# Identity matmuls in TensorE's pauses: around the chunk stage, the meta tile and the first pair of the up projection

## The chip, the cores and the metric

The kernel runs on one core of a Trainium2 chip. The metric is the device time in microseconds; the kernel before took 3239.58 us, the median of 3 runs from 3239.42 to 3240.31. A change of the time under 0.2% (6.5 us) is about what such a measurement can't tell from none.

## The reference, cut to what matters

A decoder block over 16 meta tokens and 2048 tokens of width 1024, all in float32:

```
hn   = rms_norm(h, norm_mix_pre)
proj = hn @ w_in                                   # rwkv fields, s5 input, gates
y_a  = rwkv7(p_rwkv) @ w_branch                    # a recurrence over the tokens, 8 heads of 64
y_b  = s5(u_s5) -> glu
mix  = (gate_a * y_a + gate_b * y_b) @ w_out
h    = h + rms_norm(mix, norm_mix_post)
hn   = rms_norm(h, norm_ffn_pre)
up   = hn @ ffn_w_up                               # 1024 x 5632
f    = (gelu(causal_conv(up[:, :2816])) * up[:, 2816:]) @ ffn_w_down
h    = h + rms_norm(f, norm_ffn_post)              # the 16 meta rows are dropped
```

The change leaves all of this as it is. What it adds is multiplied into PSUM places that nothing reads.

## The kernel before, in words

The program has one instruction stream for each engine; semaphores order them, and the loops are unrolled by hand at their ends. Large matmuls have their operands split in a high and a low part (float32r) and take three products, hi x hi, hi x lo, lo x hi. Small ones, and TensorE's transposes with the identity `ident` (128x128, float32), work in plain float32.

The stages, with the stretch of the profile that each takes:

- the input projection (`norm_in_projection`, to 958 us), which ends with a gate tile: weight tiles against all tokens, small matmuls of the rwkv fields and of the s5 scan between them. `tile_loop` is its loop; its last argument is a tail.
- the chunks (`rwkv_chunks`, 959 to 1427 us): the recurrence in 33 chunks of 64 tokens, two at a time in 17 steps. TensorE's part first prepares chunk 0 alone: `grams_of`, `gram_l`, `turn_toks`, a transpose `turn_x1`, a product `lx`, and then `levels`, in which `xq`, `turn_x` and `lx` alternate, each waiting for VectorE or ScalarE to copy or scale what the one before put into PSUM. Then comes step 0, written out (it has chunk preparations of both lanes, `pres`, and one main chunk), a loop over 15 steps, and a last step with no preparations (`if not pres`), in which `main_...` products and transposes of the result (`turn_y`) wait for VectorE and ScalarE in turn.
- the mix of the two branches (`branch_mix`, from 1428 us); its first products are of the chunk stage's result, and VectorE multiplies each with a gate, at L2322.
- the output projection (`token_projection`, to 1918 us), in row tiles of 128 tokens and at last a meta tile of 16. `turn` transposes a normed row tile, for the next stage.
- the up projection (`ffn_up`, from 1919 us), by pairs of weight tiles. Each pair is seven products, `for step in range(7)`, in the order P_1, P_2, P_6, P_7, P_4, P_5, P_3; in the first phase each has three units of 258, 256 and 512 columns, of 12 matmuls each. In the first pair VectorE and ScalarE still split the activations (L2999 and L3152) while TensorE works. After the first pair come 10 more of that phase, then the second phase, then the down projection.

Three things set the order around the change. TensorE takes its instructions in order: a matmul that is put ahead of a waiting one delays it if it lasts longer than the wait. A block of the program (`nc.Block()`) ends when every engine has drained (DRAIN in the profile, which ends with the engine's last instruction), and behind it `stage_ends` clears semaphores behind a second barrier (L3711 and L3713). And several lines that the prediction speaks of belong to one helper: L1537 is `products`, L1543 is `turns`, L1565 is `grams_of`, L2567 is `turn`, L2966, L2969 and L2972 are the three products of a unit of up.

```
mm = T_.transpose(psum[:, first + b, place * WIDE:(place + 1) * WIDE], src(b), ident)      # turns
mm = nc.tensor.matmul(psum[0:H, 4, g * P:(g + 1) * P], b_s[:, g, :], out_1[:, g, 0:C * H], start=True, stop=True)   # tables, L544
```

Of the kernel before, what the change touches and what calls it, by code (L numbers as in the profile page):

```python
# [28 lines left out]
P = 128  # L29
# [58 lines left out]
TWO_PI_PARTS = two_pi_parts()  # L88

# [12 lines left out]
def norm_in_projection(nc, name, sems, psum, src, gain_rows, x_hi, x_lo, weight, consts, w_tiles, mu, s5_small, s5_bc, s5_tab, s5_u, s5_y, rwkv_out, gate_out, ident, pre,  # L102
# [42 lines left out]
    with ExitStack() as ctx:  # L145
# [357 lines left out]
        def _(pe):  # L503
# [201 lines left out]
            tile_loop(pe, tile, lambda: None, gate_tile, lambda: None)  # L705
# [602 lines left out]
def rwkv_chunks(nc, name, sems, psum, prep, v_dram, chunk_decay, masks_dram, bonus_dram, gate_dram, cols, y_hi, y_lo, last_roles_stored, store_last_y, last_y_stored, ident, next_loads, next_split):  # L1308
# [13 lines left out]
    with ExitStack() as ctx:  # L1322
# [182 lines left out]
        def _(pe):  # L1505
# [165 lines left out]
            def step(g, mains, pres):  # L1671
# [4 lines left out]
                has_pb = not isinstance(g, int) or g >= 1  # L1676
                if not pres:
                    main_y_state(g, 0, flat_copied(a - 2))
                    main_u(g, 0)
                    main_m(g, 0, ALL)  # L1680
                    main_y_values(g, 0, ALL)
                    main_w_values(g, 1)
                    main_w_state(g, 1)
                    turn_y(pb, copied(y_ready, a))
                    main_y_state(g, 1, flat_copied(pb))
                    main_u(g, 1)
                    main_y_values(g, 1, ALL)
                    turn_y(a, copied(y_ready, b))
                    turn_y(b, flat_copied(a))
                    return  # L1690
# [18 lines left out]
                if has_a:  # L1709
                    main_m(g, 0, ALL)  # L1710
                lx(*place[0], 0)
                if has_a:
                    main_y_state(g, 0, toks_copied(1))
                turn_x1(*place[1])
                if has_a:
                    main_y_values(g, 0, ALL)
                lx(*place[1], 0)
# [31 lines left out]

            pe.wait_ge(masks_loaded, 16)  # L1750
# [3 lines left out]
            chunk_0 = (1, 0)  # L1754
            turn_x1(*chunk_0)
            lx(*chunk_0, 0)
            levels({1: chunk_0}, lambda l, chain: None, FIRST_LEVELS)
# [596 lines left out]
def token_projection(nc, name, sems, psum, acts, first_col, w_dram, k_tiles, passes, gain, residual, out, out_first, meta_tile, next_norm=None, early=None, begun=None):  # L2354
# [23 lines left out]
    with ExitStack() as ctx:  # L2378
# [169 lines left out]
        def _(pe):  # L2548
            pe.sem_inc(k_done, k_tiles)
            for part in range(passes):  # L2550
# [11 lines left out]
                def turn(s, r, u, i, n, token):  # L2562

                    pe.wait_ge(row_normed, r + 1 + SLOTS)
                    pe.wait_ge(turned_out, r + 1)
                    for k in range(KD):
                        mm = nc.tensor.transpose(psum[:, 4 + 2 * u + k // 4, k % 4 * P:k % 4 * P + n], row_normed_buf[0:n, u, k * P:(k + 1) * P], ident[0:n, 0:n])  # L2567
                    mm.then_inc(turned, 1)

                if next_norm:  # L2570
                    pe.sem_inc(turned, SLOTS)
                    products(0, 0, 0, 0, P, 0)
                    pe.wait_ge(*mix_banks_free)
                    tiles(pe, products, turn, part)
                else:
                    tiles(pe, None, products, part)
# [149 lines left out]
def ffn_up(nc, block, name, sems, psum, x_space, x_raw, w_raw, w_sets, x_rest, x_sums, conv_w, conv_b, hidden_out, ahead):  # L2726
# [13 lines left out]
    with ExitStack() as ctx:  # L2740
# [206 lines left out]
        def _(pe):  # L2947
            pe.sem_inc(c21_done, 3)
            pe.sem_inc(c12_done, 3)

            def pair(phase, m, first, last, extra):
                g, u0, n = pair_of(phase, m), units_before(phase, m), n_units(phase)
                for step in range(7):
                    for v, part, c0, c1 in units(phase):
# [6 lines left out]
                        cols = slice(c0 - first_column(phase), c1 - first_column(phase))  # L2961
                        pe.wait_ge(freed, count)
# [716 lines left out]
def hybrid_block(nc, ins, out):  # L3679
# [18 lines left out]
    with ExitStack() as ctx:  # L3698
# [54 lines left out]
        with ExitStack() as both:  # L3753
# [4 lines left out]
            with ExitStack() as inner:  # L3758
# [42 lines left out]
                with nc.Block() as block:  # L3801
                    up_done = ffn_up(nc, block, "up", sems, psum, x_space, x_raw, up_weight, ins["w_up_sets"], h_normed, up_sums,
                                     cols[:, COL["conv_w"]:COL["conv_w"] + CONV_W * M_FF], cols[:, COL["conv_b"]:COL["conv_b"] + M_FF], hidden,
                                     (first_set_loaded, held_a, held_b, hidden_sums, down))
                    ffn_down(nc, block, "down", sems, psum, down, *up_done, ins["ffn_post"], h1, out)
# [66 lines left out]
```

## Time and profile before

| | |
|---|---|
| median of 3 runs | 3239.58 us |
| profiled execution, its own time | 3237.82 us |
| its span, first to last instruction | 3236.0 us |
| TensorE busy | 3081.9 us, 95% |
| TensorE weight loads busy | 2751.7 us, 85% |
| VectorE, ScalarE, GpSimd busy | 1986.8, 1346.1, 114.5 us |
| mean granted TensorE clock | 0.984 |

The span and the time differ by 1.8 us, which lie around the first and last instruction. TensorE's share of busy time is the modelled length of its matmuls, which overlap. The clock that TensorE is granted has two levels in this trace, 1.00 (2.4 GHz) and 0.50 (1.2 GHz); at the half level each column takes twice the time. The mean of 0.984 is made of eleven stretches at 0.50 within the span and one at its end.

### The profile page before, as it was taken

The numbers are of one execution on the slowest core, as the hardware profiler recorded it, in microseconds if no ns is written. First come the engines' busy times: TensorE is split into PE (matmuls) and PEld (weight loads), VectorE is DVE, ScalarE is ACT, GpSimd is POOL, SyncE is SP. The second block draws the span as 40 slices with busy tenths as digits, with TensorE's granted clock in tenths as the row PEclk, the third lists the DMA queues.
The fourth block names the chain that finished last, engine by engine and source line by source line (L and its number), as shares of the span: only waits on it lengthen the run. The fifth ranks groups of instructions, "written<-read, shape, count | busy, mean of one in ns | idle before, by whom it ended". The sixth has DMA issues, their size and how long they took to land. (4 is left out here: it accounts for less than half of the span.)

```text
span 3236.0 us, 69046 instructions
## 1 busy us (share of the span) xinstructions
PE 3081.9 (95%) x25426; PEld 2751.7 (85%) x25426; DVE 1986.8 (61%) x3726; ACT 1346.1 (42%) x2373; POOL 114.5 (4%) x120
## 2 busy tenths in 40 slices
PE   8999999999987888869999979999999999999999
PEld 7999999999976777759998868999988888788877
DVE  7676655655654666654345467666687767645576
ACT  6211127667662444441113335444454444433333
POOL 0000000000001222210000000000000000000000
PEclk9999999999998999989999989999999999999999
DMA  5343346566553343333345723333354444666785
GB/s 160 112 140 120 125 154 199 188 199 192 187 149 74 88 100 91 94 116 130 127 143 177 225 101 101 108 108 106 98 166 125 125 126 120 199 219 223 246 308 188
DMA packets 448438, 481.91 MB, mean 149 GB/s; under 512 B 145552, under 2 KB 370704, under 8 KB 444352
## 3 DMA queue, kind: packets, MB, share of 16 engines
q1 hardware_dynamic: 447264, 480.30, 47.4%
q8 instruction: 71, 1.16, 0.2%
q14 instruction: 47, 0.39, 0.0%
q10 hardware_dynamic: 1056, 0.07, 0.0%
HBM read 315.36 MB, written 164.89 MB: 148 GB/s over the span
## 5 line engine op out<-in xcount | busy, mean ns | idle before, releaser
L3480 PE MATMUL psum<-down_w_parts,down_a_hi 128*128 128x512 f32 x1232 | 382.2, 391 | 6.9 <-DVE down_a_lo L3587 6.9
L2966 PE MATMUL psum<-up_x,up_w_hi 128*128 128x512 f32 (+2 forms) x1540 | 353.7, 352 | 12.1 <-ACT up_w_hi L2987 7.0
L2972 PE MATMUL psum<-up_x,up_w_hi 128*128 128x512 f32 (+2 forms) x1540 | 352.8, 351 | 0.8 <-DVE up_x L3152 0.8
L2969 PE MATMUL psum<-up_x,up_w_lo 128*128 128x512 f32 (+2 forms) x1540 | 351.9, 351 | 0.0
L2966 PEld LDWEIGHTS psum<-up_x,up_w_hi 128*128 128x128 f32 x1540 | 260.4, 190 | 53.7 <-issue 7.1
L2969 PEld LDWEIGHTS psum<-up_x,up_w_lo 128*128 128x128 f32 x1540 | 260.5, 190 | 40.7
L2972 PEld LDWEIGHTS psum<-up_x,up_w_hi 128*128 128x128 f32 x1540 | 260.0, 190 | 41.3 <-DVE up_x L3152 1.1
L3480 PEld LDWEIGHTS psum<-down_w_parts,down_a_hi 128*128 128x128 f32 x1232 | 232.3, 189 | 56.9 <-issue 8.7
L697 PE MATMUL psum<-x_hi,proj_w_hi 128*128 128x416 f32 (+1 forms) x640 | 245.1, 383 | 0.0
L3480 PE MATMUL psum<-down_w_parts,down_a_lo 128*128 128x512 f32 x616 | 240.7, 391 | 0.0
L580 PE MATMUL psum<-x_hi,proj_w_hi 128*128 128x416 f32 (+1 forms) x640 | 224.7, 351 | 0.0
L697 PE MATMUL psum<-x_lo,proj_w_hi 128*128 128x416 f32 (+1 forms) x640 | 223.6, 349 | 0.0
L580 PE MATMUL psum<-x_hi,proj_w_lo 128*128 128x416 f32 (+1 forms) x640 | 223.4, 349 | 0.0
L580 PE MATMUL psum<-x_lo,proj_w_hi 128*128 128x416 f32 (+1 forms) x640 | 223.4, 349 | 0.0
L697 PE MATMUL psum<-x_hi,proj_w_lo 128*128 128x416 f32 (+1 forms) x640 | 223.2, 349 | 0.0
L3135 DVE TENSOR_TENSOR up_w_lo<-up_weight,up_w_hi 128x512 fp32r<-128x512 f32 x176 | 118.9, 686 | 93.8 <-ACT up_w_hi L2987 93.8
L3587 DVE TENSOR_TENSOR down_a_lo<-down_raw,down_a_hi 128x1408 fp32r<-128x1408 f32 x54 | 87.7, 1624 | 123.0 <-ACT down_a_hi L3511 122.9
L3511 ACT ACTIVATE down_a_hi<-down_raw 128x1408 fp32r<-128x1408 f32 x54 | 74.5, 1380 | 175.0 <-PE psum L3480 142.9
L2987 ACT ACTIVATE up_w_hi<-up_weight 128x512 fp32r<-128x512 f32 x176 | 109.7, 624 | 85.0 <-PE psum L2972 78.7
L814 ACT ACTIVATE proj_pre<-psum 128x416 f32<-128x416 f32 (+1 forms) x70 | 36.1, 517 | 258.6 <-PE psum L580 204.1
L2987 ACT ACTIVATE up_w_hi<-up_t_sums 128x512 fp32r<-128x512 f32 x132 | 82.8, 629 | 138.7 <-PE psum L2972 129.5
L3480 PEld LDWEIGHTS psum<-down_w_parts,down_a_lo 128*128 128x128 f32 x616 | 116.4, 189 | 24.4
(422 smaller groups left out, 6533.2 us busy)
## 6 DMA issues: line engine op xcount, KB each, us to landing
down_raw<-scratch_hidden SPq DMA_DIRECT2D x48, 704.0 KB, 6.3
scratch_hidden<-up_hidden SPq DMA_DIRECT2D x44, 512.0 KB, 3.2
up_weight<-in_w_up_sets SPq DMA_DIRECT2D x42, 512.0 KB, 4.7
up_weight<-in_w_up_sets SPq DMA_DIRECT2D x84, 256.0 KB, 3.5
proj_scan_area<-scratch_s_tab SPq DMA_DIRECT2D x32, 608.5 KB, 3.9
scratch_s_tab<-proj_area SPq DMA_DIRECT2D x16, 1089.0 KB, 4.3
proj_weight<-in_w_in_tiles SPq DMA_DIRECT2D x33, 512.0 KB, 4.5
down_raw<-scratch_hidden_sums SPq DMA_DIRECT2D x24, 704.0 KB, 5.7
```

Of the source, the lines that this page charges most:

```text
L580: mm = nc.tensor.matmul(psum[:, PRODUCT_BANKS[n], 0:WIDTHS[n]], w[:, v, k, :], x[:, k, block_of(n)], start=(k == 0 and w is w_hi and x is ...
L697: mm = nc.tensor.matmul(psum[:, GATE_BANKS[n], 0:WIDTHS[n]], w[:, v, k, :], x[:, k, block_of(n)], start=(k == 0 and w is w_hi and x is x_h ...
L814: nc.scalar.activation(pre[:, 2 + STARTS[n]:2 + STARTS[n] + WIDTHS[n]], done, ACT.Copy).then_inc(evacuated, 1)
L2966: nc.tensor.matmul(out, w_hi[:, q % 7, k, :], x_hi(phase, step)[:, k, cols], start=opens and k == 0, stop=False, skip_group_check=True)
L2969: nc.tensor.matmul(out, w_lo[:, q % 7, k, :], x_hi(phase, step)[:, k, cols], start=False, stop=False, skip_group_check=True)
L2972: mm = nc.tensor.matmul(out, w_hi[:, q % 7, k, :], x_lo(phase, step)[:, k, cols], start=False, stop=closes and k == K4 - 1, skip_group_che ...
L2987: nc.scalar.activation(w_hi[:, q % 7], weight_of(part, step), ACT.Copy).then_inc(w_hi_ready, 1)
L3135: V.tensor_tensor(w_lo[:, q % 7], weight_of(part, step), w_hi[:, q % 7].bitcast(F32), ALU.subtract).then_inc(w_lo_ready, 1)
L3480: return nc.tensor.matmul(bank, a[:, q % SLOTS, k, :], w(step_of(q), k), start=opens, stop=closes, skip_group_check=True)
L3511: nc.scalar.activation(a_hi[:, q % SLOTS], raw(q, 0), ACT.Copy).then_inc(acts_hi, 1)
L3587: V.tensor_tensor(a_lo[:, q % SLOTS], raw(q, 0), a_hi[:, q % SLOTS].bitcast(F32), ALU.subtract).then_inc(acts_lo, 1)
```

## The change

One helper, `turn_over`, issues `n` matmuls of the identity by itself: 128 rows, 128 columns, float32. It is called

- as the tail of the projection's loop: 22
- at the start of the chunk stage: 28; behind `turn_toks` of chunk 0: 14; behind its `turn_x1` and `lx`: 4 each; and 4 behind each of the eight calls of `fill` in `levels`
- in step 0 alone (where `has_a` is false): 6, 8 and 6
- in the last step of the chunks: 4, 9, 4, 4, 6, 18 and 32
- ahead of the meta tile's transposes: 42, and behind them, as the last of the output projection: 16
- at the start of up: 18, and in its first pair ahead of the fourth product (P_1 + 3, which is P_7), unit 0: 20

There is no new wait, no DMA, and nothing on other engines.

```diff
+def turn_over(nc, out, ident, n):
+
+    for _ in range(n):
+        nc.tensor.matmul(out, ident, ident, start=True, stop=True)
...
-            tile_loop(pe, tile, lambda: None, gate_tile, lambda: None)
+            tile_loop(pe, tile, lambda: None, gate_tile, lambda: turn_over(nc, psum[:, ROLE_BANKS[0], 2 * P:3 * P], ident, 22))
...
+                between = lambda n: turn_over(nc, psum[:, 0, 2 * P:3 * P], ident, n)
+                first_idle = lambda n: turn_over(nc, psum[:, WUM_BANKS, 2 * P:3 * P], ident, n)
                 if not pres:
                     main_y_state(g, 0, flat_copied(a - 2))
                     main_u(g, 0)
+                    between(4)
                     main_m(g, 0, ALL)
                     main_y_values(g, 0, ALL)
                     main_w_values(g, 1)
                     main_w_state(g, 1)
+                    between(9)
                     turn_y(pb, copied(y_ready, a))
+                    between(4)
                     main_y_state(g, 1, flat_copied(pb))
                     main_u(g, 1)
+                    between(4)
                     main_y_values(g, 1, ALL)
+                    between(6)
                     turn_y(a, copied(y_ready, b))
+                    between(18)
                     turn_y(b, flat_copied(a))
+                    between(32)
                     return
...
                 if has_a:
                     main_m(g, 0, ALL)
+                else:
+                    first_idle(6)
                 lx(*place[0], 0)
                 if has_a:
                     main_y_state(g, 0, toks_copied(1))
+                else:
+                    first_idle(8)
                 turn_x1(*place[1])
                 if has_a:
                     main_y_values(g, 0, ALL)
+                else:
+                    first_idle(6)
                 lx(*place[1], 0)
...
+            between = lambda n: turn_over(nc, psum[:, 0, 2 * P:3 * P], ident, n)
+            between(28)
             pe.wait_ge(masks_loaded, 16)
             grams_of(1, 0)
             gram_l(1)
             turn_toks(1)
             chunk_0 = (1, 0)
+            between(14)
             turn_x1(*chunk_0)
+            between(4)
             lx(*chunk_0, 0)
-            levels({1: chunk_0}, lambda l, chain: None, FIRST_LEVELS)
+            between(4)
+            levels({1: chunk_0}, lambda l, chain: between(4), FIRST_LEVELS)
...
                 def turn(s, r, u, i, n, token):
 
+                    if n < P:
+                        turn_over(nc, psum[:, 3, 0:P], ident, 42)
                     pe.wait_ge(row_normed, r + 1 + SLOTS)
                     pe.wait_ge(turned_out, r + 1)
...
                     tiles(pe, products, turn, part)
+                    turn_over(nc, psum[:, 3, 0:P], ident, 16)
...
             pe.sem_inc(c12_done, 3)
+            turn_over(nc, psum[:, 7, 0:P], ident, 18)
...
+                        if first and phase == FIRST and step == P_1 + 3 and v == 0:
+                            turn_over(nc, psum[:, 7, 0:P], ident, 20)
                         pe.wait_ge(freed, count)
```

## Rows read from the trace of the kernel before

**Rows 1.** Windows cut at the clock's changes: length, busy of each engine, clock, DMA.

```profile
991.42:1005.07 13.65, 12.46 (x290) 10.63 (x284) 3.19 (x11) 3.07 (x8) 0.00 (x0) 0.50 0.39 81
...
1032.38:1035.79 3.41, 3.41 (x74) 2.96 (x73) 0.86 (x3) 2.07 (x6) 0.00 (x0) 0.50 0.14 31
...
1414.67:1431.74 17.07, 6.65 (x46) 5.61 (x47) 7.41 (x18) 10.87 (x27) 0.00 (x0) 0.50 0.14 42
```

**Rows 2.** Float32 matmuls: by line (ns min/median/max), timeline (start us, us, records).

```profile
L544 PE MATMUL psum<-proj_area x64: 272/273/283, 118.4 to 450.0; 128*16 128x128 f32 x64
...
118.36 0.61 PE L544 MATMUL psum<-proj_area 128*16 128x128 f32 x4
...
954.24 0.60 PE L568 MATMUL psum<-proj_scan_area 128*128 128x258 f32 x2
```

**Rows 3.** Drain (ns; first, last start); timeline at the chunks' start (bracket: idle before).

```profile
L145 SPq DRAIN  x1: 7/7/7, 957.8 to 957.8; - x1
...
959.21 1.28 ACT L1911 ACT_TABLE_LOAD   x1 [3.05 <-PEq L3713]
...
964.29 1.99 PE L1565 MATMUL psum<-chunk_pre 64*64 64x128 f32 x32 [9.45 <-DMA chunk_pre<-scratch_roles]
...
969.95 0.44 PE L1543 MATMUL psum<-ident_sb,chunk_x 128*128 128x128 f32 x2 [2.03 <-DVE chunk_x L1784]
...
980.98 1.99 PE L1565 MATMUL psum<-chunk_pre 64*64 64x128 f32 x32 [0.47 <-PEq L1760]
```

**Rows 4.** Timeline of TensorE: step 0 of the chunks, and a step of the loop.

```profile
990.04 0.44 PE L1543 MATMUL psum<-ident_sb,chunk_x 128*128 128x128 f32 x2 [1.67 <-DVE chunk_x L1784]
991.04 0.43 PE L1537 MATMUL psum<-chunk_x,chunk_l_t 64*64 64x32 f32 x16 [0.56 <-ACT chunk_x_t L1928]
...
1011.08 1.10 PE L1565 MATMUL psum<-chunk_pre 64*64 64x128 f32 x32
...
1204.42 0.43 PE L1537 MATMUL psum<-chunk_x,chunk_l_t 64*64 64x32 f32 x16 [0.59 <-ACT chunk_x_t L1928]
...
1220.00 1.10 PE L1565 MATMUL psum<-chunk_pre 64*64 64x128 f32 x32
```

**Rows 5.** End of the chunks and start of the mix: timeline, and a drain.

```profile
1405.29 0.59 PE L1537 MATMUL psum<-chunk_m,chunk_ar 64*64 64x64 f32 x11 [5.85 <-issue]
...
1407.02 0.51 PE L1537 MATMUL psum<-chunk_toks_held 64*64 64x64 f32 x8 [0.61 <-ACT chunk_u L1943]
...
1420.85 0.69 PE L1543 MATMUL psum<-ident_sb,chunk_y_unit 128*128 128x128 f32 x2 [2.54 <-DVE chunk_y_unit L1846]
...
L1322 DVEq DRAIN  x1: 458/458/458, 1425.9 to 1425.9; - x1
...
1432.59 0.59 DVE L2322 TENSOR_TENSOR mix_mixed<-psum,mix_gate 128x416 f32<-128x416 f32 x1 [6.24 <-PE psum L2231]
```

**Rows 6.** The meta tile: timeline, and the drains that end its block.

```profile
1906.66 1.03 PE L2567 MATMUL psum<-ident_sb,mixout_row_normed_buf 128*128 128x128 f32 x8
...
1913.74 1.03 PE L2567 MATMUL psum<-ident_sb,mixout_row_normed_buf 16*128 16x16 f32 x8 [6.04 <-DVE mixout_row_normed_buf L2686]
...
L3779 PEldq DRAIN  x1: 1058/1058/1058, 1913.8 to 1913.8; - x1
...
L3779 SPq DRAIN  x1: 7/7/7, 1918.2 to 1918.2; - x1
```

**Rows 7.** The first pair of up: timeline, and one window (columns as in Rows 1).

```profile
1924.63 1.23 PE L2972 MATMUL psum<-up_x,up_w_hi 128*128 128x258 f32 x4 [0.83 <-DVE up_x L3152]
...
1940.61 1.23 PE L2966 MATMUL psum<-up_x,up_w_hi 128*128 128x258 f32 x4 [2.89 <-ACT up_a_pre L3008]
...
1947.79 0.65 PE L2966 MATMUL psum<-up_x,up_w_hi 128*128 128x258 f32 x4
...
1967.21 0.90 PE L2966 MATMUL psum<-up_x,up_w_hi 128*128 128x258 f32 x4 [2.22 <-DVE up_a_pre L3172]
...
1930.00:1940.00 10.00, 7.72 (x45) 6.48 (x43) 9.91 (x9) 3.32 (x4) 0.00 (x0) 1.00 0.00 0
```

More of the change, by code:

```diff
@@ L2723, in _, with ffn_up @@
                     channels_out(TILES, 0, TILES // 2, N_META)
-def ffn_up(nc, block, name, sems, psum, x_space, x_raw, w_raw, w_sets, x_rest, x_sums, conv_w, conv_b, hidden_out, ahead):
+def ffn_up(nc, block, name, sems, psum, ident, x_space, x_raw, w_raw, w_sets, x_rest, x_sums, conv_w, conv_b, hidden_out, ahead):
     first_set_loaded, held_a, held_b, hidden_sums, down = ahead
@@ L3801, in hybrid_block @@
                 with nc.Block() as block:
-                    up_done = ffn_up(nc, block, "up", sems, psum, x_space, x_raw, up_weight, ins["w_up_sets"], h_normed, up_sums,
+                    up_done = ffn_up(nc, block, "up", sems, psum, ident, x_space, x_raw, up_weight, ins["w_up_sets"], h_normed, up_sums,
                                      cols[:, COL["conv_w"]:COL["conv_w"] + CONV_W * M_FF], cols[:, COL["conv_b"]:COL["conv_b"] + M_FF], hidden,
```

## The prediction

> **What bounds the kernel now.** I read the page first: a span of 3236.0 us beside an own time of 3237.82 us, with TensorE busy for 95% of it. TensorE is the bound nearly everywhere, so two things matter: where it pauses, and where its clock is at the half level. The second I read from windows cut at the clock's changes [rows 1]. There are eleven stretches at 0.50 within the span; by the mean clock of 0.984 they are some 2 x 0.016 x 3236 = 100 us together. Eight lie in the three places of the change: four at the start of the chunks, two at their end, two in the first pair of up. The other three lie later, from 1967 us on, with no identity matmul near them. Third, I read the timeline of these places for what each pause waits for [rows 3 to 7], because a clock that stays full is worth something only where TensorE's own work sets the end.
>
> What a half clock costs here is not half of 100 us. Much of those stretches is pause: in 1414.67 to 1431.74 us TensorE is busy for 6.65 of 17.07 us [rows 1]. The stretch that is worth most is 991.42 to 1005.07 us, busy for 12.46 of 13.65 us.
>
> **The price of one identity matmul.** Float32 matmuls that are no transposes make two records each. Two of them with 128 moving columns make four records; their modelled length together is 0.61 us and that of a single record 0.27, so that the starts are (0.61 - 0.27)/3 = 0.11 us apart [rows 2]. That is two cycles of 2.4 GHz for a column (128 x 2 / 2.4 = 107 ns). I take 0.218 us for one identity matmul at full clock and 0.43 at half. All 297 of them make 65 us of TensorE time, against pauses that hold less in most places. The bounds for one: 0.107 us below, if it made one record as a transpose does, and 0.43 above.
>
> The Trainium skill, page "TensorE: Matmul & The Clock Gate", section "Back-to-back issue gap", gives about 81 ns for each matmul in a sustained stream of weight load and matmul at 128 columns. For two records that makes an estimate of 0.162 us, by which the sum below would come to about -8 us in place of +7. The trace's four records are 0.11 us apart and not 0.08; the measurement decides.
>
> **The change part by part** (plus is later than before; times of before on the left).
>
> *End of the projection, 22.* TensorE's last matmul starts at 954.24 + 0.22 = 954.46 us (the second of two records, of 258 columns) [rows 2]. 22 x 0.218 = 4.8 us behind it end at 959.6. The block waits for all engines; the last is now SyncE's queue at 957.8 us [rows 3]. TensorE becomes the last: +1.9 us, and all loads of the chunk stage start that much later. If an identity matmul cost 0.14 us, this would be nothing.
>
> *Start of the chunks, 28.* The stage begins at 959.2 us, by ScalarE's first instruction, and TensorE waits until 964.29 for a DMA [rows 3], a pause of 5.1 us. 28 x 0.218 = 6.1 us: +1.0.
>
> *Chunk 0 alone, 14 and ten times 4.* From its start to `turn_x1` it takes 969.95 - 964.29 = 5.66 us [rows 3], at half clock and with a pause of 2.03 us. At full clock the same 54 records take about 2.1 us (between half of the 3.6 ahead of the pause and the whole; the grams alone are 1.10 in place of 1.99 long), and 14 x 0.218 = 3.05 fill more than the pause: 5.15, -0.5. From there to step 0 it is 980.98 - 969.95 = 11.03 us, in ten links, the pauses in which are about 0.5 us long with 0.3 of the last matmul's length to them. 4 x 0.218 = 0.87 us is a little over what a link waits, and the last two groups of 4 lie together. I make it 11.3: the clock gives 1.5 us and the overshoot takes it back. +0.3.
>
> *Step 0: 6, 8, 6.* Up to its product `lx` of lane 1 it takes 991.04 - 980.98 = 10.06 us. The faster first part gives 1.6 us, 20 x 0.218 = 4.4 us stand against pauses of 1.67 and 0.56 us [rows 4] and the ends of the matmuls ahead, 2.6 together, and take 1.8: +0.2. From that product to the next step it takes 1011.08 - 991.04 = 20.04 us, in the loop 1220.00 - 1204.42 = 15.58 us at full clock with the same work and one pair of transposes more [rows 4]. Some 0.7 us of the difference are a pause of another kind (issue): -3.7. This is the main gain of the change.
>
> So the chunk stage's start: 1.9 + 1.0 - 0.5 + 0.3 + 0.2 - 3.7 = -0.8 us.
>
> *Last step of the chunks.* The pause of 5.85 us ahead of 1405.29 us is "issue" and not a wait [rows 5]; it comes ahead of the first identity matmul of this step, so nothing fills it and the clock falls as before. Behind it 4 identity matmuls at half clock, 1.7 us, stand against a pause of 0.61 us and the last matmul's 0.3: +0.8. The four eights of `main_y_values` at full clock give 0.9 back; the chain of VectorE ahead of the last transposes moves with the first delay, and 18 x 0.218 = 3.9 us against 2.54 + 0.4 take 1.0. With 0.8 for the 9, 4, 4 and 6 the last transposes start +1.7. The block then ends with VectorE's drain at 1425.9 + 0.46 = 1426.4 us, 5.5 us behind them; 0.2 + 32 x 0.218 + 0.2 = 7.4 us: +1.9. The mix starts at full clock. VectorE waits 6.24 us for its first product [rows 5], 12 matmuls of 416 columns, 4.2 us at half clock (416 / 1.2 GHz each) and 2.1 to 2.3 at full; with a chance of a fall in the 2 us between, -1.5. Sum: +2.1.
>
> *The meta tile, 42 and 16.* The pause is 6.04 us, from 1907.5 to 1913.74 [rows 6]. 42 x 0.218 = 9.2 us end at 1916.7. Eight transposes take 0.8 us, then 16 x 0.218 = 3.5, and TensorE drains at 1921.25. Its drain now begins at 1913.8 and takes 1.06 us; SyncE's is last, at 1918.2 us, for a store that does not depend on the meta tile. That cover of 3.3 us is used up: +3.05, and all of up starts later by it.
>
> *Start of up, 18.* They take 3.9 us from about 1919.6 (1918.2 and what lay between drain and first instruction at the chunks, 1.4 us [rows 3]) and end at 1923.5; the 8 matmuls of 258 columns that follow take 0.9 at full clock, until 1924.4, and TensorE waits until 1924.63 us anyway for VectorE's low part [rows 7]: 0. Faster products behind it give nothing either. Ahead of the third product TensorE pauses until 1940.61 us, and VectorE is busy for 9.91 of the 10 us before [rows 7]: VectorE sets this point, and it starts +3.05 late. TensorE comes there sooner than now, so the pause grows from 3 to 6 us, with no identity matmul in it. The clock falls, for longer than the present 3.4 us: +1.0 (0 to 1.8).
>
> *First pair, 20.* They stand ahead of the fourth product, which begins at 1947.79 us with no idle time in front [rows 7]. Up to 1965 us TensorE doesn't pause, and the pause ahead of 1967.21 waits for VectorE work that itself follows TensorE's fifth product. So 20 x 0.218 = +4.4 us, in full. What would hide it: a pause that moves there from the third product, which I don't see.
>
> *Falls of the clock elsewhere.* The one at 1032.38 us [rows 1], the one behind the pause of 2.22 us ahead of 1967.21 [rows 7] and a later one follow pauses much shorter than those of the stage ends. Each costs up to 1.7 us (half of 3.41). After a shift some will not come, and others may: -2.3, between -5 and +2.
>
> Sum: -0.8 + 2.1 + 3.05 + 1.0 + 4.4 - 2.3 = +7.4 us (rounded), 3245.3 us on the profiled execution's 3237.82, and 3247.0 on the median, 1.8 us above it.
>
> **The rivals.**
> *The overshoots hide.* The added time at the block ends and in the first pair might meet slack that I haven't seen (ScalarE's and VectorE's queues behind the third product). Without the 4.4 and half of the barriers' 6.8 it would be about 0 us: 3239.6. For it speaks that VectorE and ScalarE wait for each other in the first pair; against it that TensorE runs without a stop from 1940.61 to 1965 us.
> *An identity matmul costs about 0.14 us: faster.* 42, 20, 18 and 14 of them divide the pauses of 6.04, 2.89, 2.54 and 2.03 us at 0.14 us each. The place is the meta tile: under 6.2/42 = 0.147 us no overshoot is left there, nor at the block ends. Then the start of the chunks gives 7.9 us (3.7, 1.6, and 2.6 of chunk 0), their end 3, the 20 cost 2.8 plus 1.0 of clock, and the 2.3 of falls elsewhere stay: -9 us, 3230.2. Against it speak the four records [rows 2].
> *The clock isn't held.* If identity matmuls don't keep it full, each overshoot is doubled and no gain is left: 12 to 25 us more, 3256.
> *The change holds the clock, but to no use,* because VectorE's and ScalarE's chains set the chunk stage's start: without the 3.7 us it is +11, 3250.6, in the range of the forecast.
>
> **How the numbers follow.** The forecast, overshoots in full (with the last rival), 0.60, its own range 3242 to 3252; the hidden overshoots 0.20; the cheap matmul 0.13; the clock not held 0.07. The range reaches from 3234 to 3252 us: above, the sum with its worst bounds; below, the hidden overshoots with luck at the clock. Under 0.2% (6.5 us) lies what a measurement can't tell from no change. Of the forecast's 0.60 some 0.43 lie over it and 0.17 within; with the others: faster 0.13, within 0.36, slower 0.51.
>
> **What the profile after would show.** The two records of an identity matmul 0.107 to 0.11 us apart; TensorE's drain the last at all three block ends; no half clock from 957 to 1030 us, and about 16 us from `lx` to step 1; the clock low behind the loop's end as before; a pause of some 6 us ahead of up's third product, and 20 identity matmuls between its third and fourth with ScalarE and VectorE idle behind. I am wrong if the records come faster, if a block's drain doesn't wait for them, or if the loop's steps change.

## The result: slower by 0.29%

The changed kernel took 3246.08 us, the median of 9 runs from 3241.47 to 3249.83; the kernel before took 3236.87 beside it (9 runs, 3231.63 to 3240.93). The ratio is 1.0029, with a 95% interval of 1.0020 to 1.0037: +9.2 us, forecast +7.4. Of all executions timed for this text one was slow, with 10567.62 us in the run `e10_behind8` below; without it the median of that kernel is 3234.25 us.

The profiled execution of after took 3241.47 us, the shortest of its nine, with a span of 3239.6 us. Against the trace of before it is only 3.6 us longer, and the reason lies where nothing was changed: after is 1.3 us ahead when the projection ends, and gets 4.1 us back behind up's first pair. By the starts of VectorE's instructions it is 7.5 us behind at 2868 us of before, 5.8 at 3119 and 3.7 at 3186. There before has a fall of the clock at 3131.58 us that none of the other traces has; why the distance shrinks ahead of it too is not shown. What lies between is read from milestones: differences of starts in the timeline of each kernel.

| us | before | after | difference | forecast |
|---|---|---|---|---|
| last product of the projection to the chunk stage's first instruction | 4.75 | 6.75 | +2.0 | +1.9 |
| from there to the first grams (28) | 5.08 | 6.46 | +1.4 | +1.0 |
| first grams to `turn_x1` (14) | 5.66 | 5.10 | -0.6 | -0.5 |
| `turn_x1` to step 0 (ten 4s) | 11.03 | 13.29 | +2.3 | +0.3 |
| step 0 to `lx` of lane 1 (6, 8, 6) | 10.06 | 10.52 | +0.5 | +0.2 |
| `lx` of lane 1 to step 1 | 20.04 | 17.43 | -2.6 | -3.7 |
| step 1 | 30.94 | 27.57 | -3.4 | -1.7 (as a fall elsewhere) |
| the loop, to the last step's first product | 357.11 | 356.42 | -0.7 | 0 |
| last step to its last transposes | 21.71 | 24.90 | +3.2 | +1.7 |
| last transposes to the mix's first product | 7.56 | 9.57 | +2.0 | +1.9 |
| mix's first product to VectorE's work at 1447.58 (before) and 1447.67 us (after) | 19.17 | 16.46 | -2.7 | -1.5 |
| last full transposes to up's first instruction (42, 16) | 11.79 | 15.07 | +3.3 | +3.05 |
| up's first instruction to its eighth product (18, 20) | 55.29 | 58.52 | +3.2 | +5.4 |

They add up to +7.9 us. A new fall of the clock at 1706 us adds 1.1: +9.0. The mix's -2.7 is in two parts. VectorE's first gate comes 2.67 us behind TensorE's first product in place of 4.18, which is the clock's gain of 1.5. The other 1.2 vanish in a wait: before, VectorE is idle for 1.52 us ahead of 1447.58 us until ScalarE has written `mix_w_hi`, and in after it has no idle time there. The last row's +3.2 holds a gain that is no work of the change: the fall of the clock at the seventh product (1967.6 us of before) did not come, and the seventh product takes 5.81 us in place of 7.29.

The identity matmuls in the timeline of after:

```profile
953.41 5.07 PE L94 MATMUL psum<-ident_sb 128*128 128x128 f32 x44
...
966.41 1.10 PE L1571 MATMUL psum<-chunk_pre 64*64 64x128 f32 x32
...
971.51 0.38 PE L1549 MATMUL psum<-ident_sb,chunk_x 128*128 128x128 f32 x2
971.73 1.06 PE L94 MATMUL psum<-ident_sb 128*128 128x128 f32 x8
...
984.80 1.10 PE L1571 MATMUL psum<-chunk_pre 64*64 64x128 f32 x32
```

44 records in 5.07 us, a single one 0.27 long: (5.07 - 0.27)/43 = 0.112 us apart, so 0.22 us for one identity matmul, as forecast. The grams take 1.10 us in place of the 1.99 of before [rows 3]: the clock is full there.

The drains at the three block ends, each from the answer for the line of its block:

```profile
L151 PEldq DRAIN  x1: 2173/2173/2173, 956.3 to 956.3; - x1
L151 SPq DRAIN  x1: 7/7/7, 957.1 to 957.1; - x1
...
L1328 DVEq DRAIN  x1: 458/458/458, 1425.3 to 1425.3; - x1
L1328 PEldq DRAIN  x1: 2173/2173/2173, 1427.0 to 1427.0; - x1
...
L3811 SPq DRAIN  x1: 7/7/7, 1919.4 to 1919.4; - x1
L3811 PEldq DRAIN  x1: 2173/2173/2173, 1920.5 to 1920.5; - x1
```

TensorE is the last at all three: 956.3 + 2.17 = 958.5 us against SyncE's 957.1, 1429.2 against VectorE's 1425.8, 1922.7 against SyncE's 1919.4. Before it was never the last [rows 3, 5, 6].

The timeline behind: step 0's issue pause, the last step, the mix, and up's first pair.

```profile
1003.18 0.84 PE L1543 MATMUL psum<-chunk_q,chunk_x_t 64*64 64x32 f32 x21 [0.95 <-issue]
...
1403.00 0.70 PE L1543 MATMUL psum<-chunk_w,chunk_x_held 64*64 64x64 f32 x16 [5.80 <-issue]
1403.64 2.07 PE L94 MATMUL psum<-ident_sb 128*128 128x128 f32 x8
...
1421.86 7.31 PE L94 MATMUL psum<-ident_sb 128*128 128x128 f32 x64
...
1433.88 0.59 DVE L2348 TENSOR_TENSOR mix_mixed<-psum,mix_gate 128x416 f32<-128x416 f32 x1 [8.14 <-PE psum L2257]
...
1945.12 1.23 PE L2998 MATMUL psum<-up_x,up_w_hi 128*128 128x258 f32 x4 [5.29 <-ACT up_a_pre L3040]
...
1952.51 4.63 PE L94 MATMUL psum<-ident_sb 128*128 128x128 f32 x40
1956.89 0.74 PE L2998 MATMUL psum<-up_x,up_w_hi 128*128 128x258 f32 x4
...
1976.43 0.75 PE L2998 MATMUL psum<-up_x,up_w_hi 128*128 128x258 f32 x4 [2.22 <-DVE up_a_pre L3204]
```

The reader is to see four things. The issue pause behind the loop is what it was (5.80 and 5.85). The pause ahead of up's third product has grown from 2.89 to 5.29 us, and that product starts 21.4 us behind up's first instruction in both kernels, so VectorE and ScalarE set it. 40 records stand between the third and the fourth product with no pause on either side. And the pause of 2.22 us ahead of the seventh product is the same as before [rows 7]: nothing of the 20 is hidden there.

Windows cut at the clock's changes (length, busy of PE, PEld, DVE, ACT, POOL, clock, DMA):

```profile
957.00:1003.20 46.20, 42.30 (x732) 38.99 (x730) 12.62 (x37) 8.35 (x15) 5.99 (x9) 1.00 0.43 87
1003.24:1006.66 3.42, 3.42 (x75) 2.97 (x79) 0.57 (x2) 0.77 (x2) 0.00 (x0) 0.50 0.02 5
...
1706.39:1709.80 3.41, 3.41 (x9) 2.68 (x9) 3.25 (x6) 0.15 (x1) 0.00 (x0) 0.50 0.47 185
1941.91:1948.74 6.83, 3.62 (x17) 3.62 (x18) 6.83 (x12) 4.57 (x9) 0.00 (x0) 0.50 0.22 54
```

The clock is full for the 46 us in which it was low for 37 before, and falls behind a 0.95 us issue pause. At up's third product the low stretch has doubled to 6.83 us, but 3.2 us of it are pause. It does that in the traces of `e9_small8` and `e10_behind8` below as well, which have nothing of the change in up.

### The profile page after: what moved, and what is told of

Read it like the earlier page. It is cut to its first block and busy times, and to the rows that moved or that the text cites. A ratio compares the mean times of both kernels' runs of the same rounds, so it can differ in the third digit from the quotient of the medians.

```text
span 3239.6 us, 70234 instructions
## 1 busy us (share of the span) xinstructions
PE 3127.7 (97%) x26020; PEld 2802.5 (87%) x26020; DVE 1986.5 (61%) x3726; ACT 1344.7 (42%) x2373; POOL 114.4 (4%) x120
## 3 DMA queue, kind: packets, MB, share of 16 engines
q8 instruction: 75, 1.23, 0.2%
```

## The experiments

All were timed in five rounds beside the kernel before. First the parts: one left out, and the two halves alone.

**Without the 20** (`e1_no20`, a count of 0).

```diff
-                            turn_over(nc, psum[:, 7, 0:P], ident, 20)
+                            turn_over(nc, psum[:, 7, 0:P], ident, 0)
```

> The changed kernel without the 20 identity matmuls in up's first pair. Theory (identity matmuls last longer than the pauses they stand in): the fourth product follows the third without a gap again, and the time is 3 to 4.4 us under the changed kernel's, so 5 to 6 us over the kernel before. The pause of 2.2 us in front of the seventh product, which is gone in the changed kernel, comes back; by its size the gain is nearer 3.2 than 4.4. Rival (the 20 are hidden behind VectorE's work, and up's loss comes from its late start and low clock): the time stays that of the changed kernel, within 1 us, and the stretch from the third product to the eighth keeps its length.

Measured: 3245.25 us against 3237.78, ratio 1.0024 (1.0015 to 1.0033). From up's first instruction to the eighth product it takes 54.99 us (before 55.29; the changed kernel 58.52), so that leaving out the 20 saves 3.5 us in the trace. The expectation is wrong about the pause: 2.22 us ahead of the seventh product stand in all three traces. The clock makes the rest. From the third to the fourth product it takes 7.18 us before, 11.76 in the changed kernel and 8.36 here: the 20 cost their 4.4 us in full, and here the low clock reaches 5.8 us behind the start of the third product in place of 3.6, which costs 1.0. The seventh product takes 7.29, 5.81 and 5.79 us, because the clock falls there in before alone. That 54.99 is near 55.29 is luck. The time fell less, 7.5 in place of 9.2 us over before, but the two intervals leave room for either.

**The chunks' parts alone** (`e2_chunks_only`: 0 for 42, 16, 18 and 20).

> Only the parts of the change around the chunk stage (projection's end, chunks' start, step 0, last step); none at the meta tile and in up. Theory: the shifts between the two traces are +2.0 us at the projection's end, -2.7 to the loop, +2.5 from the loop's end to the mix, so about +2 us over the kernel before, and from the meta tile on everything as before. Rival (the loss is not local, but comes from falls of the clock that moved, as the new one at 1706 us): the time is as far over the kernel before as the whole change's, or under it, and doesn't follow the places.

Measured: 3239.99 against 3237.78 us, ratio 1.0007 (0.9998 to 1.0016): +2.2, which the interval doesn't tell from nothing. Meta tile and up are those of before (11.78 and 55.41 us).

**The other parts alone** (`e3_rest_only`: 0 for all those of projection and chunks).

> Only the parts at the meta tile and in up (42, 16, 18 and 20); none around the chunks. Theory: +3.3 us at the meta tile's barrier and +3.2 us in up's first pair, so 6.5 us over the kernel before; with the run without these parts it adds up to the whole change's +9. Rival (falls of the clock elsewhere make the loss): no such sum, and the difference shows at places without identity matmuls.

Measured: 3243.16 us, ratio 1.0015 (1.0006 to 1.0024): +5.4, with 15.07 and 58.51 us in the two places, as in the changed kernel. 2.2 + 5.4 = 7.6, within the error of 9.2: the loss is local.

**Counts fitted to the pauses** (`e4_fitted`).

The counts are those of the expectation; two edits are more than a number:

```diff
-            levels({1: chunk_0}, lambda l, chain: between(4), FIRST_LEVELS)
+            levels({1: chunk_0}, lambda l, chain: between(0 if l == 2 and chain is not lx else {lx: 2, xq: 2, turn_x: 3}[chain]), FIRST_LEVELS)
...
-                        if first and phase == FIRST and step == P_1 + 3 and v == 0:
-                            turn_over(nc, psum[:, 7, 0:P], ident, 20)
+                        if first and phase == FIRST and step == P_1 + 2 and v == 0:
+                            turn_over(nc, psum[:, 7, 0:P], ident, 28)
```

> The same places, with as many identity matmuls as the pause holds at 0.218 us each, read from the changed kernel's trace: 14 for 22, 22 for 28, 10 for 14, 2 to 3 for each 4 and none behind the last link of chunk 0, 0, 2, 3 for 6, 8, 6 in step 0, 1, 4, 3, 2, 1, 10, 16 for 4, 9, 4, 4, 6, 18, 32 in the last step, 28 and 14 for 42 and 16, 10 for 18, and in up's first pair 28 ahead of the third product in place of 20 ahead of the fourth. Theory (the clock's part is a gain, the overshoot is the whole loss): the start of the chunks 11 to 12 us shorter than in the changed kernel, their end 6 to 7, the meta tile's barrier 3.3, up 3 to 4; together 14 to 20 us under the kernel before, with the clock full in all these places but behind the 5.8 us issue pause. Rival A (the clock is held only by the surplus): it falls in the short pauses again, and the time is that of the kernel before within 3 us. Rival B (VectorE's and ScalarE's chains set these stages): pauses take the place of the surplus, the clock stays full, and the time is 0 to 8 us under the kernel before.

Measured: 3229.17 us, ratio 0.9972 (0.9961 to 0.9983), -8.6: faster, by half of what was expected, and not where it was expected. Chunk 0 from first grams to step 0 takes 13.35 us (before 16.69, after 18.39), but the two steps behind it take 62.93 (61.05, 55.52), with more issue pauses, and the clock falls behind the first of them:

```profile
995.57 0.26 PE L1543 MATMUL psum<-chunk_m,chunk_ar 64*64 64x64 f32 x1 [2.73 <-issue]
...
1002.00 0.45 PE L1543 MATMUL psum<-chunk_x,chunk_l_t 64*64 64x32 f32 x9 [1.59 <-issue]
```

From the last step to the mix's first gate on VectorE it takes 29.72 us in place of 33.46, and there the pause of 5.8 us is gone: one of 1.75 stands ahead of 1407.89 us. Nothing in the counts explains that. That raised a new theory: issue pauses are waits for TensorE's own instructions. DMA queues in two windows of before, ahead of 1402.4 us and behind it:

```profile
q1 hardware_dynamic: 1402, 0.93, 105.6%
...
q8 instruction: 1, 0.02, 13.3%
```

In the first 2.9 us of the pause (1399.5 to 1402.4 us) the instruction queue moves nothing; nor does it from 1042 us on, in the whole loop. Its packet starts between 1402.4 and 1403, and TensorE goes on at 1405.29. Between 980.98 and 1042.02 us the queue has 10 packets. The page gives 71 packets and 1.16 MB for before, 75 and 1.23 MB for after: 16.4 KB each, and four more for the 70234 - 69046 = 1188 instructions of 297 identity matmuls, four each. The two halves of the change, with 804 and 384 instructions, have 74 and 72 packets, so that the queue is TensorE's.

The Trainium skill, page "Runtime: NRT & Kernel Launch", sections "Terms" and "What's in a NEFF", has an instruction memory for each engine that is refilled in 16 KiB blocks, and instructions of 64 bytes: 256 in a block. The trace agrees with the size of the block.

**Only the edges moved** (`e5_align8`: nothing of the change, but 8 in place of 28 at the chunk stage's start).

```diff
+            between(8)
             pe.wait_ge(masks_loaded, 16)
```

> The kernel before with one thing added: 8 identity matmuls at the start of the chunk stage, where TensorE waits 5 us for a DMA, so that they cost nothing; they are 32 instructions, and move all later instructions of TensorE by as many. Theory (the issue pauses are waits for 16 KB blocks of TensorE's instructions, and where they fall goes by where the block's edges lie): the pause of 5.85 us behind the loop's end falls to 1 to 3 us, as in the fitted kernel, whose 70 identity matmuls ahead of it are 280 instructions, 24 more than one block of 256; in the changed kernel they are 124, 496 instructions, 16 less than two blocks, and its pause stayed 5.80. The time is then 3 to 5 us under the kernel before. Rival (the fitted kernel's short pause came from its full clock or its faster start): the pause stays at 5.8 us, and the time that of the kernel before within 1 us.

Measured: 3229.72 against 3236.48 us, ratio 0.9976 (0.9966 to 0.9987), -6.8. The timeline behind the loop:

```profile
1396.71 0.46 PE L1543 MATMUL psum<-chunk_m,chunk_ar 64*64 64x64 f32 x16 [1.11 <-ACT chunk_flat L1987]
1398.33 0.35 PE L1543 MATMUL psum<-chunk_toks_held 64*64 64x64 f32 x7 [0.93 <-ACT chunk_u L1969]
1400.67 0.46 PE L1543 MATMUL psum<-chunk_toks_held,chunk_grams_held 64*64 64x64 f32 x16 [0.63 <-POOL chunk_toks_held L2102]
1403.29 0.68 PE L1543 MATMUL psum<-chunk_m,chunk_ar 64*64 64x64 f32 x16 [2.15 <-issue]
```

TensorE comes two waits further (0.93 and 0.63) on what it still holds, and the pause is 2.15 us in place of 5.85. From the last step to the mix's gate it takes 28.50 us in place of 33.46; another 2.1 us are gained from the stage's start to step 2. These eight gave most of what the fitted kernel's 187 gave.

**Fitted, with the old edges** (`e6_fit_realign`: the fitted kernel with 16 in place of 22).

> The fitted kernel with 16 in place of 22 identity matmuls at the start of the chunk stage, in a pause that holds either: 64 of them ahead of the loop's end, 256 instructions, just one block. Theory (edges of instruction blocks): the pause behind the loop's end is 5.8 us again, and the time some 4 us over the fitted kernel's, 4 to 5 us under the kernel before. Rival (clock and surplus decide): the pause stays 1.75 us, and the time that of the fitted kernel, 8.6 us under the kernel before.

Measured: 3231.87 us, ratio 0.9984 (0.9975 to 0.9993), -4.6. The pause is back:

```profile
1407.29 0.38 PE L1543 MATMUL psum<-chunk_m,chunk_ar 64*64 64x64 f32 x4 [5.78 <-issue]
```

and from the last step to the mix's gate it takes 32.75 us, nearly the 33.46 of before. Whether the time follows, the two intervals leave open, since they overlap. What is left of the gain is in chunk 0 (13.19 us in place of 16.69), as far as the trace shows.

**Edges and the fitted last step** (`e7_end_only`).

> The kernel with 8 identity matmuls at the start of the chunk stage (32 instructions, as in the run with these alone) and the fitted counts in the last step of the chunks (1, 4, 3, 2, 1, 10, 16); nothing else of the change. Theory: the shorter issue pause gives 3 to 4 us and the full clock from the last step to the mix 1.5 to 2.5 more, 5 to 6 us under the kernel before in all, 1.5 to 2 under the run with the 8 alone. Rival (all of the fitted kernel's gain at this place is the pause, and the clock gives nothing because VectorE's and ScalarE's chain sets the last step): no difference to the run with the 8 alone.

Measured: 3230.39 us, ratio 0.9977 (0.9968 to 0.9986), -6.1: no difference to the 8 alone, as the rival has it. The stretch takes 31.04 us with a pause of 2.32, against 28.50 with the 8 alone: in the traces the fitted counts lose 2.5 us here, and the clock doesn't give them back.

**64 columns** (`e8_cols64`).

```diff
-        nc.tensor.matmul(out, ident, ident, start=True, stop=True)
+        nc.tensor.matmul(out[:, 0:64], ident, ident[:, 0:64], start=True, stop=True)
```

> The changed kernel with all its counts, but each identity matmul multiplies only 64 of the 128 columns. Its count of instructions and so all block edges are those of the changed kernel. Theory (the overshoot is the loss): an identity matmul takes some 0.11 to 0.13 us in place of 0.218, no place but the six of step 0 overshoots any more, the meta tile's 42 end ahead of VectorE, the 20 cost half; 9 to 12 us under the changed kernel if the clock holds, so 0 to 3 us under the kernel before. Rival A (two weight loads of 128 columns set the price, not the columns): the records stay 0.109 us apart, and the time is that of the changed kernel, 7 to 9 us over the kernel before. Rival B (half the columns don't hold the clock): records 0.055 us apart, and the clock falls in the pauses as in the kernel before; the time is that of the kernel before or up to 3 us over it.

Measured: 3251.14 us, the median of 7 runs from 3246.59 to 3286.23, ratio 1.0043 (1.0029 to 1.0057), +14.7: above what each theory says. The profiled execution took 3271.43 us, 20.3 over this median. Its timeline, and a window:

```profile
958.04 5.02 PE L94 MATMUL psum<-ident_sb 128*128 128x64 f32 x44
964.56 12.03 PE L94 MATMUL psum<-ident_sb 128*128 128x64 f32 x56 [1.50 <-PEq L3745]
```

```profile
964.73:1012.52 47.79, 47.79 (x372) 46.17 (x372) 6.65 (x19) 3.25 (x5) 4.18 (x7) 0.50 0.25 44
```

44 records still take 5.02 us (5.07 with 128 columns), so the columns don't set the price: rival A is right. And in this execution the clock fell at 964.73 us and stayed low for 47.79 us, in which TensorE was busy without a break; in the four traces with the 128-column counts there (after, `e1`, `e2`, `e12`) it stayed full. The 28 then take 12.03 us in place of 6.49, and from the stage's start to step 0 it takes 20 us more than in the changed kernel. That is as much as this execution took over the median. The median run has a mean clock of 0.990, by which some 65 us were at the half level (2 x 0.010 x 3249, an estimate), against some 105 us in the profiled one with 0.984. So the long low stretch can't be what most executions had, and rival B is shown for this one alone. What lifts the median from rival A's 7 to 9 us to 14.7 is not shown; its interval overlaps that of the changed kernel.

**The 8 without work** (`e9_small8`: 8 multiplications of 16x16, the same 32 instructions).

> As the run with 8 identity matmuls alone, but each of them multiplies 16x16 in place of 128x128: 32 instructions with hardly any work. Theory (they only move the edges of TensorE's instruction blocks): the pause behind the loop's end is 2.0 to 2.5 us as there, and the time 6 to 8 us under the kernel before. Rival (the work of the identity matmuls, by the clock, made the gain): the pause is 5.8 us again, and the time within 1.5 us of the kernel before.

Measured: 3233.11 against 3236.70 us, ratio 0.9989 (0.9980 to 0.9997), -3.6, and a pause of 2.70 us ahead of 1409.27. The pause is short again, so it is the instructions and not their work. The time is less good than forecast; the intervals of the two runs overlap. In the traces chunk 0 takes 17.13 us against 14.97 with the large ones. There the clock is at the half level without a break from 958.54 us for 30.72 us, while with the large ones it is full between 963.81 and 970.65 us. So of the 6.8 us of the large ones about 2 seem to be the clock's in chunk 0; from the last step to the mix's gate the two kernels are alike (29.37 and 28.50 us).

**The 8 behind the loop** (`e10_behind8`: `between(8)` behind `turn_y(b, ...)`).

> The 8 identity matmuls (128x128) stand behind the last transposes of the chunk stage, so behind the loop's end, where VectorE's drain hides their 1.7 to 3.5 us; nothing else of the change. Theory: up to there all block edges are those of the kernel before; the pause stays 5.8 us, and the time within 2 us of the kernel before. Rival (any place will do, because the gain came from the clock or from another alignment than the loop's end): 6 us under it.

Measured: 3235.24 us (3234.25 without its one long execution), ratio 0.9998 (0.9989 to 1.0007): no change. The pause stands at the same instruction as in before, but is 3.94 us long. With the same edges it was 3.93 in the run of the meta tile's and up's parts. So the edges set where it is; how long it lasts varies by 2 us.

**20 in place of 8** (`e11_plus20`).

> 20 in place of 8 identity matmuls at the start of the chunk stage: 80 instructions, 4.4 us in the 5.1 us pause. Theory: in all runs so far the first block behind the loop is fetched 4.4 to 5.2 us after the loop's end, wherever the edges lie; what the edges set is how many instructions TensorE still has until then. Here it has 48 fewer than with the 8, so the pause begins sooner and is 2.5 to 4.5 us; the time is 3 to 6 us under the kernel before. Rival (only the position of the edge within a few instructions counts): as with 8, or the full 5.8 us.

Measured: 3232.17 us, ratio 0.9986 (0.9977 to 0.9994), -4.5, and a pause of 3.37 us ahead of 1406.14, 23 matmul records earlier in the program than with the 8. That is what 48 instructions make, at a weight load and a matmul each (24): the edge moves as the count says. The sentence on the fetch "4.4 to 5.2 us behind the loop's end in all runs" was wrong when written: in the run of the meta tile's and up's parts it was 3.0. Over all runs it is 2.6 to 5.6, from the end of the loop's last transposes.

**The changed kernel with the edges moved** (`e12_after38`: 38 in place of 28).

> The changed kernel with 38 in place of 28 identity matmuls at the start of the chunk stage: 134 ahead of the loop's end, 536 instructions, 24 more than two blocks, as in the fitted kernel. Theory: the pause behind the loop falls from 5.8 to some 2 us, which gives 4 to 6 us, and the 10 more cost up to 2.2: 2 to 5 us under the changed kernel, so 4 to 7 over the kernel before. Rival (the overshoots take it, since in this kernel TensorE's own work sets the last step): the pause falls, and the time is that of the changed kernel or more.

Measured: 3247.89 us, ratio 1.0032 (1.0021 to 1.0042), +11.2: the rival. The pause fell to 1.55 us (ahead of 1409.60), and from the last step to the mix's gate it takes 34.22 us in place of 37.14, but the start of the stage pays 2.2 us for the ten, steps 0 and 1 take 59.16 us in place of 55.52, and up's eighth product comes 60.03 us behind its start in place of 58.52, because the clock falls at the seventh here. The time itself can't be told from that of the changed kernel.

The stretches of all kernels with comparable code, in us:

| | stage's start to step 2 | last step to the mix's gate |
|---|---|---|
| starts of before (before, `e3`, `e10`) | 82.81, 83.60, 82.38 | 33.46, 32.37, 32.51 |
| starts of after (after, `e1`, `e2`) | 80.37, 85.49, 82.13 | 37.14, 38.03, 37.00 |
| 8, small 8, 20, 8 with fitted end | 80.69, 84.52, 85.31, 82.71 | 28.50, 29.37, 29.98, 31.04 |
| fitted, fitted with old edges | 81.39, 82.55 | 29.72, 32.75 |
| the changed kernel with 38 | 86.24 | 34.22 |

Whatever is put into the start of the stage, step 2 comes 80 to 86 us later (107.17 in the profiled execution with 64 columns, left out of the table), and the same code (after, `e1`, `e2`) spreads over 5 us. The second column is tight and follows the edges.

Two more readings of all fourteen traces bear the theory out. First, the pause behind the loop ends 2.3 to 2.9 us after the start of a packet of the instruction queue in every one. Second, its place goes by the count. Between the loop's last transposes and the pause stand 3 matmul records in before, `e3` and `e10`, and 9 in `e6` (a whole block more); 16 in after, `e1`, `e2` and `e8` (496 instructions more); 89 in `e11` (80 more); 112 or 113 in `e5`, `e7` and `e9` (32 more); 122 in `e4` and `e12` (24 over one block and over two). From before's 3, with two instructions a record and 256 a block, the counts give 3, 11, 91, 115 and 119.

## Why the prediction was right, and where not

**The sum.** The range held, and the sign and the size are right: +7.4 forecast, +9.0 by the milestones, +9.2 by the medians. The likeliest case, overshoots in full, is what happened. That the terms add up so well is in part luck: the gain forecast for the start of the chunk stage is not there in the mean of three kernels, and a fall of the clock less in up made good for it in this trace.

**The price.** 0.218 us was forecast and 0.22 measured. The estimate from the Trainium skill's 81 ns (page "TensorE: Matmul & The Clock Gate", section "Back-to-back issue gap"), and with it the rival of the cheap matmul, falls. The reason I gave, two cycles for a column, falls too: 64 columns cost the same. The weight loads, two for each identity matmul, are left as the likely cause; that is argued, not shown.

**Block ends.** +1.9, +1.9 and +3.05 forecast; +2.0, +2.0 and +3.3 measured, TensorE's drain last each time. The best steps of the prediction.

**Chunk 0's links.** The term that was mis-sized: "I make it 11.3", +0.3; it took 13.29, +2.3. The product behind a group of 4 starts 0.4 to 0.65 us after the end of what it waits for. ScalarE's copy, for example, started at 971.93 and took 0.38 us, while the product that waits for it came at 972.71. The last eight, 1.8 us, stand where TensorE paused 0.47 us before [rows 3].

**Step 0 and the clock.** "No half clock from 957 to 1030 us" was wrong, by one fall of 3.4 us behind an issue pause. The gain from `lx` to step 1 was 2.6 us and not 3.7, and step 1 gave 3.4. But as a steady gain this step fails: in the two other kernels with the same start, steps 0 and 1 together take 60.64 and 57.28 us against 55.52, and before 61.05. I put the pauses down as "a pause of another kind (issue)", 0.7 us, and took them as fixed. They are waits for instructions: the pauses ahead of 996.32, 1026.50 and 1032.28 us of before end 2.3 to 2.5 us after the start of a packet too. 10 blocks pass in these two steps, and a TensorE that gets there sooner waits longer for the next one (4.3 us in all before, 2.5 in after, 6.9 in the fitted kernel): the fitted kernel gained 3.3 us in chunk 0 and lost 1.9 in the steps. In the mean of three kernels each, the stage's start gives 0.3 us, against the 2.7 forecast (-0.8, of which the block's end is +1.9).

**Last step.** The issue pause stayed, as forecast, and the clock low behind it. The overshoots were +3.2 and not +1.7, the block's end +2.0 against +1.9. The mix's full clock gave the 1.5 of the forecast, and 1.2 more vanished in a wait for ScalarE; together +2.5 against +2.1. That gain is not steady either: VectorE's gate comes 2.67 us behind the mix's first product in after and `e2`, but 3.90 in `e1` and 4.22 in `e12`, against 4.18 before. What the prediction missed is that this pause, 5.85 us, was the largest thing to be had here, and that the number of identity matmuls ahead of it decides on it. The change has 124, 496 instructions, and by chance leaves the edges within 16 instructions of where they were.

**Meta tile.** +3.3 against +3.05, and the same 15.07 us in every kernel that has the 42 and 16 (within 0.1 with 64 columns).

**Up.** "So 20 x 0.218 = +4.4 us, in full" and +1.0 for the clock: +5.4 against +3.2. The first step held: the fourth product comes 4.6 us later, and the pause ahead of the seventh product is 2.22 us long with and without the 20, as it should be if VectorE's work there follows TensorE's fifth product. The term that was mis-sized is the clock's +1.0. It came to 0.2 to 0.3: the low stretch grew by the pause, and without the 20 third to fourth product would take 7.4 us against 7.18. In `e1`, where the low clock reached further, it came to 1.2. The rest, -1.5, is the fall at the seventh product that did not come, and belongs to the next term.

**Falls elsewhere.** -2.3 forecast. The ones at 1032 and 1967 us did not come, one at 1706 us did. The one at 1967 us is not the change's doing: `e9` and `e10`, with the up projection of before, don't have it either, and `e12`, with that of the changed kernel, has it. For the others it was not settled.

**Rivals.** The hidden overshoots, the cheap matmul and the clock not held are refuted for this kernel. The clock not held came true in the profiled execution with 64 columns. The fourth, that the change holds the clock to no use, fits the start of the chunk stage best, with 0.3 us in the mean; but what stands in the way there is the waits for instructions, and not only the chains of VectorE and ScalarE that it names.

## What to carry to other kernels

Work that fills a pause of TensorE must end before the wait does, and at a block's end before the engine that is now last; in the changed kernel's trace the places that lost came to some 18 us and those that gained to some 10. But read "issue" pauses first: here, behind the exit of a loop and in code that ran for the first time with many small matmuls, TensorE waited for its own instructions, and where the blocks' edges lay decided how long. Eight matmuls in an idle place, 32 instructions, gave 6.8 us, and 3.6 with hardly any work in them; when comparing two versions of a kernel, such a shift can pass for the effect of the edit, so vary it alone.

## What the hardware showed that I had not expected

- TensorE went on 2.3 to 2.9 us after the packet with a 16 KB block of its instructions started, in all fourteen traces (1402.46 to 1405.29 us in before), and none was fetched during 360 us in the loop. The first packet came 2.6 to 5.6 us behind the loop's end.
- An identity matmul in float32 costs 0.22 us at full clock with 128 as with 64 columns (5.07 and 5.02 us for 22 of them).
- In one execution TensorE was busy for the whole of 47.79 us and was granted half the clock all the time, while it worked mostly on identity matmuls of 64 columns. The busy time of the profile didn't say whether the clock would hold.
- A long row of identity matmuls made TensorE's drain record 2.17 us long at all three block ends (1.62, 0.74 and 1.06 us before), while the drain still ends with the last matmul.
